# Decoder layer with forgetting and block attention: x loaded in 2 KB rows, first value unit in two halves

## The reference

```
h    = rms_norm(x, norm_pre_g)
proj = h @ w_in                    # 8 groups of 512 columns, and 8 forget columns
y_a  = forgetting attention (8 heads x 64, causal, bias by a cumulated log forget gate) * silu(g_a)
y_b  = block attention with ALiBi (8 heads x 64; with 256 rows there is one block) * silu(g_b)
out  = x + rms_norm(concat(y_a, y_b) @ w_out, norm_post_g)
```

## Time and profile before

| what | before |
|---|---|
| median of three runs | 145.1 us |
| time of the profiled execution | 145.13 us |
| its span, first to last instruction | 143.3 us |
| granted TensorE clock, mean | 0.992 |
| TensorE busy | 134.4 us, 94% |
| VectorE busy | 109.4 us, 76% |
| ScalarE busy | 98.7 us, 69% |
| bytes moved | 26.96 MB, 9725 packets |

### The profile page before, as it was taken

One profiled execution on the slowest core, in us unless ns is written; L12 is line 12 of the kernel. 1 busy time (PEld: TensorE's weight loads), 2 busy tenths in 40 slices (PEclk: granted clock), 3 DMA queues, 4 the chain that ended last, 5 costly groups with the idle time before them and its releaser, 6 DMA issues.

```text
span 143.3 us, 2857 instructions
## 1 busy us (share of the span) xinstructions
PE 134.4 (94%) x1076; PEld 127.4 (89%) x1076; DVE 109.4 (76%) x230; ACT 98.7 (69%) x198; POOL 40.0 (28%) x58
## 2 busy tenths in 40 slices
PE   7789999999999999999999999999999999999910
PEld 7679999999999999999999999999998888988910
DVE  0384966899999999988888977999689816471891
ACT  4376989678976398977875977778879833355740
POOL 3621100000000067000599235230735551120042
PEclk9999999999999999999999999999999999999996
DMA  4999999398865999758368603449600000000034
GB/s 110 233 313 386 401 395 342 88 375 254 271 223 172 389 392 377 278 160 238 112 230 237 213 9 142 146 166 293 280 2 0 0 0 5 0 0 0 0 149 146
DMA packets 9725, 26.96 MB, mean 188 GB/s; under 512 B 1384, under 2 KB 2416, under 8 KB 9456
## 3 DMA queue, kind: packets, MB, share of 16 engines
q1 hardware_dynamic: 9120, 25.57, 52.0%
q10 hardware_dynamic: 592, 1.22, 2.3%
HBM read 25.73 MB, written 1.06 MB: 187 GB/s over the span
## 4 chain that ended last, share of the span: by engine, by line
PE 87%; DMA 4%; issue 2%; DVE 2%; ACT 1%; POOL 1%; SPq 1%; POOLq 1%; DVEq 0%; ACTq 0%
PE bank L937 47%; PE score_banks L947 11%; PE bank L1128 7%; PE score_banks L1128 5%; PE score_banks L1033 4%; PE value_banks L947 4%; DMA raw<-in_w_units 4%; PE value_banks L1056 1%; PE value_banks L1044 1%; PE value_banks L1060 1%; PE value_banks L1045 1%; POOL x_t L366 1%; DVE h L882 1%; PE bank L1046 1%; PE value_banks L1059 1%
## 5 line engine op out<-in xcount | busy, mean ns | idle before, releaser
L615 DVE TENSOR_TENSOR w_lo<-raw,w_hi 128x1024 fp32r<-128x1024 f32 (+1 forms) x33 | 44.6, 1353 | 6.6 <-ACT w_hi L380 6.5
L380 ACT ACTIVATE w_hi<-raw 128x1024 fp32r<-128x1024 f32 (+1 forms) x33 | 34.4, 1056 | 6.5 <-DMA raw<-in_w_units 4.1
L937 PE MATMUL bank<-h_hi,w_hi 128*128 128x256 f32 x128 | 36.0, 281 | 0.0
L937 PE MATMUL bank<-h_lo,w_hi 128*128 128x256 f32 x128 | 35.6, 278 | 0.0
L937 PE MATMUL bank<-h_hi,w_lo 128*128 128x256 f32 x128 | 35.5, 278 | 0.0
L937 PEld LDWEIGHTS bank<-h_hi,w_hi 128*128 128x128 f32 x128 | 24.1, 188 | 0.4
L937 PEld LDWEIGHTS bank<-h_lo,w_hi 128*128 128x128 f32 x128 | 24.0, 188 | 0.0
L937 PEld LDWEIGHTS bank<-h_hi,w_lo 128*128 128x128 f32 x128 | 24.0, 188 | 0.0
L334 POOL TENSOR_TENSOR probs<-probs,row_inv 128x256 f32<-128x256 f32 (+1 forms) x16 | 15.7, 1005 | 27.6 <-DVE row_inv L764 27.5
L937 PE MATMUL bank<-xg_hi,w_hi 128*128 128x256 f32 x64 | 17.8, 278 | 0.0
L937 PE MATMUL bank<-xg_lo,w_hi 128*128 128x256 f32 x64 | 17.7, 277 | 0.0
(11 more groups left out here) (172 smaller groups left out, 326.5 us busy)
## 6 DMA issues: line engine op xcount, KB each, us to landing
raw<-in_w_units SPq DMA_DIRECT2D x30, 512.0 KB, 4.8
raw<-in_w_out SPq DMA_DIRECT2D x4, 512.0 KB, 3.2
h<-in_x SPq DMA_DIRECT2D x2, 512.0 KB, 8.1
y_parts<-in_w_out SPq DMA_DIRECT2D x2, 512.0 KB, 5.6
gpost_row<-in_w_out SPq DMA_DIRECT2D x2, 512.0 KB, 6.1
squares<-decay_rows_scratch ACTq DMA_DIRECT2D x1, 1024.0 KB, 5.9
x_t<-in_x SPq DMA_DIRECT2D x1, 1024.0 KB, 7.1
raw<-in_w_units SPq DMA_DIRECT2D x3, 256.0 KB, 5.2
```

Of the source, the lines that this page charges most:

```text
L380: nc.scalar.activation(w[0][:, s, 0:width], raw[:, s, 0:width], ACT.Copy).then_inc(s_hi, 1)
L615: nc.vector.tensor_tensor(w[1][:, s, 0:width], raw[:, s, 0:width], w[0][:, s, 0:width].bitcast(F32), ALU.subtract).then_inc(s_lo, 1)
L937: last = nc.tensor.matmul(dst, stationary(a, j), moving(b, j), start=n == 1, stop=n == count * len(PASSES))
```

## The change

The first four tiles of x come in two transfers of two tiles instead of four of one, so that every row of x is 2 KB. The first 512 columns of u0 come in one transfer of 2 KB rows instead of two of 1 KB rows. The order of issue becomes: x tiles 0 and 1; u0 first half; u0 second half; u1 first half; u1 second half; x tiles 2 and 3; u2; u3. What follows is issued as before. The splits and the products keep their pieces: a new table `X_BEHIND` says which tiles of x ScalarE and VectorE work on ahead of which unit, with the same grouping as before.

```diff
-X_LOADS = ((0, 1), (1, 2), (2, 3), (3, 4), (4, 6), (6, 8))
+X_LOADS = ((0, 2), (2, 4), (4, 6), (6, 8))
+X_BEHIND = ((0,), (1,), (2,), (3,), (4, 5), (6, 7))
...
             load_x(0)
-            load_values(0, 0, SEQ, s_piece_in[0])
-            load_values(0, SEQ, HALF, s_piece_in[1])
-            load_values(0, HALF, D_MODEL, s_raw_in[0])
+            for u in range(2):
+                load_values(u, 0, HALF, s_piece_in[u])
+                load_values(u, HALF, D_MODEL, s_raw_in[u])
             load_x(1)
-            load_values(1, 0, HALF, s_piece_in[2])
-            load_values(1, HALF, D_MODEL, s_raw_in[1])
             for u in range(2, RING):
-                load_x(u)
                 load_values(u, 0, D_MODEL, s_raw_in[u])
...
             for u in range(RING, V_UNITS):
-                if u < len(X_LOADS):
-                    load_x(u)
+                if u < len(X_BEHIND):
+                    load_x(u - 2)
...
-            for c, (lo, hi) in enumerate(X_LOADS):
-                act.wait_ge(s_x_in[c], 16)
-                for j in range(lo, hi):
+            for c, tiles in enumerate(X_BEHIND):
+                act.wait_ge(s_x_in[tiles[0] // 2], 16)
+                for j in tiles:
                     x_high(j)
                 if c < PIECED:
                     for lo, hi in PIECES[c]:
                         last = hi == V_WIDTH
-                        act.wait_ge(s_raw_in[c] if lo >= HALF or c == 2 else s_piece_in[2 * c + lo // SEQ], 16)
+                        act.wait_ge(s_raw_in[c] if lo >= HALF or c == 2 else s_piece_in[c], 16)
```

More of the change, by code:

```diff
@@ L159, in hybrid_layer @@
         s_raw_in = [sem(f"raw_in{s}") for s in range(RING)]
-        s_piece_in = [sem(f"first_piece_{c}_in") for c in range(3)]
+        s_piece_in = [sem(f"first_half_{u}_in") for u in range(2)]
         s_wf_in, s_wf = sem("w_f_in"), sem("forget_columns")
@@ L239, in _ @@
             for u in range(RING, V_UNITS):
-                if u < len(X_LOADS):
-                    load_x(u)
+                if u < len(X_BEHIND):
+                    load_x(u - 2)
                 else:
-                    t = u - len(X_LOADS)
+                    t = u - len(X_BEHIND)
                     sp.dma_start(x_rows[:, t, :], x[:, t, :]).then_inc(s_xrows_in[t], 16)
```

## The result

The change makes the kernel slower: 147.33 us in the median of five runs (147.15 to 147.87), against 145.02 for the kernel before in the same comparison. The ratio is 1.0149, with a 95% interval of 1.0124 to 1.0174. Every ratio in this document leaves out executions more than 1.5% above the fastest of their kernel, while a median counts all. Forecast were 144.8 us and a range up to 145.6.

The account below looks back on a forecast made before the run. TensorE's work was taken as the bound, with the gain set by how much earlier it resumes at u0's second half. 145.13 - 0.46 (earlier issue) + 0.12 (bytes ahead) = 144.79 us; range 144.1 to 145.6.

Parts of the forecast that it names:

- What bounds the kernel: TensorE's work list sets the time; its restart at 7.78 us, after a 1.4 us hole for u0's second half, is decisive.
- no later operand comes too late: Condition for an earlier restart to shorten the whole run; slack put at 0.41 us for u3 and 0.53 at u11.
- Part 1, the issue order: u0's second half becomes third transfer instead of fourth, issued at about 1.66 us instead of 2.12: -0.46 us.
- Part 2, the bytes: Ahead of u0's second half stand 512 KB in 2 KB rows instead of 384 KB in 1 KB rows: +0.12 us.
- Part 3, u3: 768 KB ahead of u3 change to 2 KB rows, so u3 can land 0.44 us earlier and a 0.34 gain passes.
- Part 4, what starts later: u0's first half lands at 4.5 us, TensorE starts about 5.2; the old 1.4 us hole before its second half covers this.
- Hidden as well: At the start, x lands some 0.3 us later, covered by a wait for the gain column lasting to 3.71 us.
- The clock: TensorE's granted clock stays 1.00, since holes are no longer than the earlier 1.36 us one: no cost.
- The slower case: x tile 1's bytes ahead of u0 cost 0.76 us at the start's rate: 145.4 to 145.9 us, chance 0.22.
- side remark: u0's first half also makes the kernel slower, but only if it lands after 5.4 us.
- The second rival: No change: queue place does not hold the last engine; u0's second half lands near 7.28, 145.0 to 145.1 us, chance 0.23.
- the unknown: How the DMA engines share the start: some were far ahead, and the last one set the landing of u0's second half.

Follow-up runs that it names:

- experiment 9: The kernel before with every tile of x a contiguous block of 128 KB in memory, order and quarters unchanged; 145.22 us, ratio 0.9989 to the kernel before.
- experiment 12: The changed kernel with x padded by two empty tiles, so its rows lie 10 KB apart instead of 8 KB; 144.45 us, ratio 0.9937 to the kernel before.
- experiment 4: The changed kernel with 20 products of ones at the start instead of 8; 147.83 us, ratio 1.0172 to the kernel before.
- experiment 5: The changed kernel with each pair of x tiles packed as one contiguous 256 KB block in memory; 144.16 us, ratio 0.9914 to the kernel before.
- experiment 3: The kernel before with x tile 1 issued right behind x tile 0, ahead of u0, start rows all 1 KB; 146.40 us, ratio 1.0052.
- experiment 1: The changed kernel with u0's first 512 columns in two quarters as before, x still in pairs; 147.54 us, ratio 1.0136 to the kernel before.
- experiment 2: The kernel before with u0's first 512 columns in one transfer, x still in single tiles; 144.46 us, ratio 0.9949.
- experiment 8: The changed kernel without the load of the forget weights, zeros written by GpSimd instead; 147.62 us, ratio 1.0149 to the kernel before.

## Why the prediction was wrong

**What bounds the kernel** held for the loss: it is made at the start and comes through to the end (2.77 us at 12 us, 2.8 in the span). For a gain the condition "no later operand comes too late" is not safe. The prediction looked at u3 and u11, but what held TensorE in experiment 9 was u1 (0.56 us), in experiment 12 u2 (0.58), and experiments 4, 5 and 9 gave back 1.0, 0.4 and 1.0 us between the first gate unit and the end.

**Part 1, the issue order,** held: u0's second half is the third transfer, and SyncE issues it at about 1.65. The profile of the changed kernel has four issues in 1.84 us:

```profile
1.18 1.84 SPq L216 DMA_DIRECT2D raw<-in_w_units  x4
```

**Part 2, the bytes, is the step that failed.** I charged x tile 1 ahead of u0 at +0.12 us, from the rates of two stretches far apart, and took the size of the rows for the only thing that sets a rate. u0's second half landed at 7.72 instead of the 6.94 forecast, +0.44 against before where the sum had -0.34. The cause is a property that no row of the profile before has by name: the rows of x lie 8 KB apart, and with two tiles of them at the head of the queue some DMA engines finish 2.3 us after the first, at a rate of 144 GB/s for the first 2.1 us. With the same transfers packed it is 241, with rows 10 KB apart 233, and the forecast's direction comes true, with more than its size: -0.9% in experiment 5, -0.6% in experiment 12, against the -0.2% forecast.

**Part 3, u3,** had the right sign and too small a size: it landed at 12.40, 1.08 us earlier, not 0.44. That the size of the rows is the reason, as the part has it, isn't shown. From 5.5 to 7.3 us the changed kernel moved 376 GB/s against 302, but experiment 3 moved 361 with the 1 KB rows of before, and experiment 5 only 305 with the 2 KB rows of the change. u3 was also issued 1.1 us earlier (at 4.34), an item that the prediction put at nothing.

**Part 4, what starts later, failed with part 2.** I put u0's first half at 4.5 and let the old hole cover it. It landed at 7.04, 2.5 us later than I had it, and the cover, good for a landing up to 5.4, was used up. Here 1.24 us of the 2.77 arise: without a hole in it u0 takes 2.93 us at the full clock (experiment 4), so to have u1 start at 9.31 as before it had to start by 6.38, and started at 7.62. "Hidden as well", said of x, was wrong in the same way: x and the gain column came 1.7 us later.

**The clock** was costed at nothing, on the ground that the holes would be no longer than 1.36 us. The step follows from part 4: the hole was 2.84 us. The other 1.53 us of the 2.77 (4.46 - 2.93) are matmuls 0.22 us apart instead of 0.12, the same 1.53 that experiment 4 showed at the first gate unit. The late start and the clock together are the loss.

**The rivals.** The slower case had 0.22, and put its place at u0's second half, at 145.5 us. Its side remark, that the same sign comes from the first half if it lands after 5.4, was the mechanism that came; the second half was no wait any more. The price lacked the clock (1.53 us), and the delay itself was put too low, so the range ended 1.7 us too low. The second rival has a sentence on latency under load: the Trainium skill (DMA: Bandwidth & Descriptors, latency and other measured facts) has 2 us at high load. No run here shows a single read's latency, and the 1.8 us between the strided and the packed landing of the same transfer (4.5 and 2.7) neither confirm that figure nor contradict it.

**What I could have read.** Transfers of the start were late with free engines: a DMA share of 0.69 and 0.84 with a low rate says that something beyond the queue's bytes sets the landing. The trace of before had the uneven engines too: nine were done with u0's second half by 5.18 us, the last at 7.29. The prediction named this as the unknown, and then took a price for it from rows at full rate.

## What to carry to other kernels

Before a load is moved to the head of a queue that is just starting, look at the distance of its rows in memory, not only at their length: 128 rows of 2 KB at a distance of 8 KB landed 1.7 to 1.8 us later here than at 10 KB or packed, and padding the array by two tiles repaired it. Split a change of this kind: one half of it (u0's first 512 columns in one transfer) was worth -0.5%, the other (x in pairs) +1.4%, and together they gave +1.5%, which hides the gain. And a delay at the start is paid twice if TensorE falls idle long enough for its clock to drop.

## What the runs showed of the hardware that was not expected

- How evenly the DMA engines finish a kernel's first transfer depended on its layout in memory: 256 KB of x in 2 KB rows kept them 2.0 to 2.4 us apart at 8 KB distance (four traces), 0.6 at 10 KB and 0.2 packed, and landed after 4.2 to 4.6, 2.8 and 2.6 to 2.7 us. Later in the queue no harm is seen at 8 KB distance: the changed kernel moved 376 to 396 GB/s from 5.5 to 11.2 us, with x tiles 2 and 3, 256 KB, in that stretch.
- With the value weights at 4 KB distance the stretch of 3.6 to 5.5 us ran at 290 GB/s, with them packed at 381 (one trace each).
- TensorE's granted clock stayed at 1.00 behind a hole of 1.36 us and fell to 0.50 behind holes of 2.84 and 2.6 us. In experiments 1 and 2 matmuls stood 0.21 us apart at the start while the clock column said 1.00. The trace's first record of the clock there is at 13.0 and 6.3 us, and until then the column shows 1.00; the distance of the matmuls is the better witness. In 11 of the 14 traces that record stands between 3.9 and 7.0 us, in the other three (experiments 1, 3 and 8, with holes of 2.1 to 2.9 us ahead of it) between 12.4 and 13.0: how long the start runs at the lower clock differs from one execution to the next.
